# A transformer kernel's first down projection as seven block products, and the split of rounding work between VectorE and GpSimd in both down projections

## What is computed

```python
u = causal_dwconv(hn @ w_up[l], conv_w[l], conv_b[l])       # 1024 x 5632
gate, val = jnp.split(u, 2, axis=-1)
f = (jax.nn.gelu(gate, approximate=True) * val) @ w_down[l] # 1024 x 2816 @ 2816 x 1024
h = h + rms_norm(f, ln_ffn_post[l])
```

## Time and profile before

| | us |
|---|---|
| median of three runs | 2977.24 |
| the profiled execution | 2978.39 |
| its span in the profile | 2976.7 |
| PE busy (matmuls) | 2862.1 |
| DVE busy | 1813.8 |
| ACT busy | 1241.5 |
| POOL busy | 621.2 |

### The profile page before, as it was taken

How to read it: one execution, slowest core, us unless ns; L and a number is a source line. 1 busy time by engine, 2 the same in 40 slices (tenths; PEclk the granted TensorE clock), 3 DMA queues, 4 the chain that set the end, 5 groups by cost and what they waited for, 6 DMA issues and landing times.

```text
span 2976.7 us, 47459 instructions
## 1 busy us (share of the span) xinstructions
PE 2862.1 (96%) x19810; PEld 2299.2 (77%) x19810; DVE 1813.8 (61%) x2296; ACT 1241.5 (42%) x1833; POOL 621.2 (21%) x302
## 2 busy tenths in 40 slices
PE   8999998989899999999899999999899999999999
PEld 6877777777688888888678867766678888888887
DVE  3156768852698889544685545565545766654636
ACT  4145545542545555421453433343433432333334
POOL 4310122221100000344151200000012122244543
PEclk9999999999999999999999999999899999999999
DMA  6433330002422222322345454436543344466664
GB/s 215 153 117 114 121 122 26 27 26 85 142 78 85 85 86 78 121 113 85 115 154 152 152 171 137 125 100 171 193 134 130 120 147 148 156 213 221 224 198 170
DMA packets 283992, 387.84 MB, mean 130 GB/s; under 512 B 12401, under 2 KB 188666, under 8 KB 283778
## 3 DMA queue, kind: packets, MB, share of 16 engines
q1 hardware_dynamic: 268802, 337.60, 35.7%
q10 hardware_dynamic: 14976, 47.19, 4.1%
HBM read 263.34 MB, written 121.41 MB: 129 GB/s over the span
## 4 chain that ended last, share of the span: by engine, by line
PE 85%; DVE 5%; DMA 4%; issue 3%; ACT 2%; SPq 1%; POOL 1%; DVEq 0%; ACTq 0%; POOLq 0%
PE ps L497 25%; PE ps L3284 17%; PE ps L3041 10%; PE ps L2814 9%; PE ps L2110 5%; PE ps L681 4%; PE ps L1530 4%; PE ps L2180 2%; PE ps L2161 2%; PE ps L2138 1%; PE ps L1593 1%; DMA kl<-qk_lo 1%; PE ps L2141 1%; SPq L2471 1%; PE ps L1571 0%
## 5 line engine op out<-in xcount | busy, mean ns | idle before, releaser
L463 POOL TENSOR_TENSOR wl<-wraw,wh 128x1024 fp32r<-128x1024 f32 x62 | 157.4, 2539 | 1119.1 <-ACT wh L458 1109.4
L497 PE MATMUL ps<-xh,wh 128*128 128x512 f32 x752 | 237.8, 398 | 5.2 <-POOL wl L463 2.3
L497 PE MATMUL ps<-xl,wh 128*128 128x512 f32 x752 | 233.7, 392 | 0.0
L497 PE MATMUL ps<-xh,wl 128*128 128x512 f32 x752 | 232.8, 391 | 0.0
L458 ACT ACTIVATE wh<-wraw 128x1024 fp32r<-128x1024 f32 x78 | 82.3, 1056 | 267.7 <-PE ps L497 206.8
L2814 PE MATMUL ps<-gb_hi,ga_hi 128*128 128x512 f32 x448 | 174.9, 390 | 1.6 <-POOL gb_lo L2805 0.8
L497 PEld LDWEIGHTS ps<-xh,wh 128*128 128x128 f32 x752 | 139.6, 189 | 46.7 <-issue 8.6
L2814 PE MATMUL ps<-gb_hi,ga_lo 128*128 128x512 f32 x448 | 174.4, 389 | 0.0
L2814 PE MATMUL ps<-gb_lo,ga_hi 128*128 128x512 f32 x448 | 174.3, 389 | 0.0
L3121 DVE TENSOR_TENSOR y<-ps,y 128x1024 f32<-128x1024 f32 x79 | 96.8, 1225 | 125.6 <-PE ps L497 125.6
L497 PEld LDWEIGHTS ps<-xl,wh 128*128 128x128 f32 x752 | 142.5, 189 | 30.3
(11 more groups left out here) (498 smaller groups left out, 7552.0 us busy)
## 6 DMA issues: line engine op xcount, KB each, us to landing
act_d<-act SPq DMA_DIRECT2D x16, 1792.0 KB, 6.6
ga_raw<-act_d SPq DMA_DIRECT2D x56, 512.0 KB, 4.0
wraw<-in_w_in SPq DMA_DIRECT2D x48, 512.0 KB, 5.0
gb_raw<-in_w_down SPq DMA_DIRECT2D x40, 512.0 KB, 4.9
r_raw<-in_w_up SPq DMA_DIRECT2D x38, 512.0 KB, 3.7
residual<-src ACTq DMA_DIRECT2D x32, 512.0 KB, 5.0
w_raw<-in_w_up SPq DMA_DIRECT2D x32, 512.0 KB, 5.1
proj<-stage SPq DMA_DIRECT2D x30, 512.0 KB, 3.0
```

The costliest lines, as they stand in the source:

```text
L463: nc.gpsimd.tensor_tensor(wl[:, s, :, :], wraw[:, s, :, :], wh[:, s, :, :].bitcast(F32), ALU.subtract).then_inc(w_lo, 1)
L497: mm = nc.tensor.matmul(ps[:, bank + h, :], w, x[:, h * HALF:(h + 1) * HALF], start=start and k == 0, stop=stop and k == 2)
```

## The change

The first down becomes seven block products. The 22 tiles of its inner dimension are 11 pairs (tile k and tile k+11), cut into six chunks of 2, 2, 2, 2, 2 and 1 pairs. That gives 7 x 6 = 42 steps, in which a full step has 24 matmuls and a product's last step 12, together 7 x 11 x 4 x 3 = 924. Steps 0 to 5 are P2, 6 to 11 P1, 12 to 17 P6, 18 to 23 P5, 24 to 29 P7, 30 to 35 P3, 36 to 41 P4. Both downs now use the same functions, and the last two steps are interleaved block by block. Further parts:

- The up's tiles are computed in the order 11, 0, 12, 1, and so on (`F1_TILE`). After each odd one GpSimd makes four 128x512 sums of the two finished tiles (`input_sums1_pool`), and `ff1_gated` waits for earlier ones. SyncE stores three plain blocks and four sums to `act1_d` (7 x 256 KB per pair of tiles, where it was 2 x 512 KB).
- In both downs VectorE makes the low half of the weights and GpSimd that of the inputs; before, it was the other way round in the second down, and GpSimd made both in the first.
- In both downs VectorE makes the weight sums of step i+1 before the low half of step i; before, in the second down, the sums of step i.
- The adding of chunks (`add_one`) falls away: a product's banks are moved out once. The last four squares of the first down are taken by ScalarE from PSUM.
- In the second down the wait for the stored inputs stands once, ahead of step 7's loads, instead of at every P2 step.

```diff
+        def down_load(sp, d, i):
+            name, c = d.steps[i]
+            n, home, loaded = d.kts[c], down_home(d, i), g_loaded[i % 4]
+            if i >= 8 or (i >= 4 and not d.later):
+                sp.wait_ge(down_done, down_done_by(d, i - 4))
...
+        def down_sums_dve(dve, d, i):
+            name, c = d.steps[i]
+            if name not in d.summed:
+                return
...
+            dve.wait_ge(g_loaded[i % 4], down_loaded_by(d, i))
+            if name == "P6":
...
+                    tt(two, raw, two, ALU.add).then_inc(g_sum, 1)
+                    dve.wait_ge(g_sum, at_sums - 1)
+                    tt(one, two, one, ALU.subtract).then_inc(g_sum, 1)
...
+        def down_hi_act(act, d, i):
+            n, home = down_kts(d, i), down_home(d, i)
+            act.wait_ge(g_loaded[i % 4], down_loaded_by(d, i))
+            g_act.done(nc.scalar.activation(home.f_hi[:, 0:n, :], home.f_raw[:, 0:n, :], ACT.Copy), "f")
+            if d.steps[i][0] in d.summed + ("P5",):
+                act.wait_ge(g_sum, down_sums_by(d, i))
+            g_act.done(nc.scalar.activation(home.d_hi[:, 0:n, :], down_weight_source(d, i)[:, 0:n, :], ACT.Copy), "d")
+        def down_lo_dve(dve, d, i):
+            n, home = down_kts(d, i), down_home(d, i)
+            g_act.wait(dve, "d", d.first + i)
+            g_dve.done(nc.vector.tensor_tensor(home.d_lo[:, 0:n, :], down_weight_source(d, i)[:, 0:n, :],
+                                               home.d_hi[:, 0:n, :].bitcast(F32), ALU.subtract), "d")
+        def down_prepare_dve(dve, d, i):
+            if i + 1 < len(d.steps):
+                down_sums_dve(dve, d, i + 1)
+            down_lo_dve(dve, d, i)
+        def down_lo_pool(pool, d, i):
+            n, home = down_kts(d, i), down_home(d, i)
+            g_act.wait(pool, "f", d.first + i)
+            g_pool.done(nc.gpsimd.tensor_tensor(home.f_lo[:, 0:n, :], home.f_raw[:, 0:n, :],
+                                                home.f_hi[:, 0:n, :].bitcast(F32), ALU.subtract), "f")
...
+        def down_products(pe, d, i):
+            name, c = d.steps[i]
+            down_ready_pe(pe, d, i)
             for b in range(4):
+                if c == 0 and name in DOWN_BEFORE:
+                    pe.wait_ge(down_added, down_added_by(d, DOWN_BEFORE[name], b))
+                down_block(d, i, b, c == 0 and name in DOWN_OPENS, c == len(d.kts) - 1).then_inc(down_done, 1)
...
+        def input_sums1_pool(pool, k):
...
+            ff1_dve.wait(pool, "m", 2 * k + 1)
+            if k:
+                pool.wait_ge(act2_stored[1], 32 * k)
...
+            s1_pool.done(tt(t1, b12, b11, ALU.subtract), "T1")
+            s1_pool.done(tt(t3, b22, b12, ALU.subtract), "T3")
+            s1_pool.wait(pool, "T1", k)
+            s1_pool.done(tt(t2, b22, t1, ALU.subtract), "T2")
+            s1_pool.wait(pool, "T2", k)
+            s1_pool.done(tt(t4, b21, t2, ALU.subtract), "T4")
...
@@ the hand-over on ScalarE
-            for m, x in enumerate("gv"):
-                ff1_tap(act, FF_TILES - 1, x)
-                first_copy(act, m)
+            ff1_tap(act, FF_TILES - 1, "g")
+            down_hi_act(act, down1, 1)
+            ff1_tap(act, FF_TILES - 1, "v")
+            down_hi_act(act, down1, 2)
             ff1_gelu(act, FF_TILES - 1)
...
@@ and on VectorE, the last pair and the first down
                 if not more:
+                    down_lo_dve(dve, down1, 0)
                 r7_outputs(dve, ring1, p)
...
+                for k, x in enumerate("gv"):
                     ff1_taps(dve, t, x)
+                    if not more:
+                        down_lo_dve(dve, down1, 1 + k)
                 ff1_gated(dve, t)
...
+            ends = down_ends(down1)
+            for i in range(3, len(down1.steps)):
+                down_prepare_dve(dve, down1, i)
+                if i - 2 in ends:
+                    for b in range(4):
+                        feature_add(dve, down1, ends[i - 2], b)
+            for m in range(4):
+                square_sum_dve(dve, 24 + m)
```

More of the change, by code:

```diff
@@ L78 @@
 U_UP2 = U_OUT2 + KT
-DOWN1 = FF_TILES // 2
-DOWN2_CHUNKS = FF2_TILES // 4
 PAIRS2 = FF2_TILES // 2
@@ new lines, in down_kts, with down_weight_loads, down_loaded_by, down_done_by @@
+        def down_kts(d, i):
+            return d.kts[d.steps[i][1]]
+        def down_weight_loads(d, i):
+            return {"P5": 0, "P6": 2}.get(d.steps[i][0], 1)
+        def down_loaded_by(d, i):
+            s = i % 4
+            whole = sum(16 * (1 + down_weight_loads(e, j)) for e in downs[:downs.index(d)] for j in range(s, len(e.steps), 4))
+            return whole + sum(16 * (1 + down_weight_loads(d, j)) for j in range(s, i + 1, 4))
+        def down_done_by(d, i, b=3):
+            return 4 * (d.first + i) + b + 1
@@ new lines, in down_added_by, with down_sums_by, down_weight @@
+        def down_added_by(d, name, b=3):
+            return 28 * downs.index(d) + 4 * DOWN_PRODUCTS.index(name) + b + 1
+        def down_sums_by(d, i):
+            before = [j for j in range(i + 1) if d.steps[j][0] in d.summed]
+            return d.sums + sum(2 if d.steps[j][0] == "P6" else 1 for j in before)
+        def down_weight(d, k, h, c):
+            r = (k * sum(d.kts) + sum(d.kts[:c])) * P
+            return d.weights[r:r + d.kts[c] * P, h * HALF:(h + 1) * HALF].rearrange("(k p) n -> p k n", p=P)
@@ new lines, in down_block @@
+        def down_block(d, i, b, start, stop):
+            name, home, n = d.steps[i][0], down_home(d, i), down_kts(d, i)
+            t = slice(b * P, (b + 1) * P)
+            f, w = (home.f_hi, home.f_lo), (home.d_hi, home.d_lo)
+            still, moving = (f, w) if d.tokens else (w, f)
+            for kt in range(n):
+                for k, (left, right) in enumerate(((0, 0), (0, 1), (1, 0))):
+                    mm = nc.tensor.matmul(ps[:, DOWN_BANK[name] + b, :], still[left][:, kt, t], moving[right][:, kt, :],
+                                          start=start and kt == 0 and k == 0, stop=stop and kt == n - 1 and k == 2,
@@ new lines, in down_sum_done, with down_ends, feature_add @@
+        def down_sum_done(eng, d, name, b):
+            last = len(d.steps) - 1
+            if name == "P4":
+                eng.wait_ge(down_done, 4 * (d.first + last - 1) + 2 * (b + 1))
+            else:
+                eng.wait_ge(down_done, down_done_by(d, d.steps.index((name, len(d.kts) - 1)), b))
+        def down_ends(d):
+            return {i: name for i, (name, c) in enumerate(d.steps) if c == len(d.kts) - 1 and name != "P4"}
+        def feature_add(dve, d, name, b):
+            row, h = DOWN_TO[name]
+            down_sum_done(dve, d, name, b)
+            part, bank = y[:, 4 * row + b, h * HALF:(h + 1) * HALF], ps[:, DOWN_BANK[name] + b, :]
+            if name in ("P2", "P6", "P5", "P4"):
+                if name == "P4":
+                    dve.wait_ge(x_sq, 24 + 4 + b + 1)
+                ins = nc.vector.tensor_copy(part, bank)
+            else:
+                dve.wait_ge(down_added, down_added_by(d, {"P1": "P2", "P7": "P5", "P3": "P6"}[name], b))
+                ins = nc.vector.tensor_tensor(part, bank, part, ALU.add)
+            ins.then_inc(down_added, 1)
@@ L3701, in _ @@
             for i in range(2):
-                g_lo_pool(pool, i)
+                down_lo_pool(pool, down2, i)
             pair_input_sums(pool, PAIRS2 - 1)
-            for i in range(2, len(DOWN2_STEPS)):
-                g_lo_pool(pool, i)
+            for i in range(2, len(down2.steps)):
+                down_lo_pool(pool, down2, i)
         @block.scalar
@@ L3923, in _ @@
                 else:
-                    g_hi_act(act, 1)
+                    down_hi_act(act, down2, 1)
                 pair_copies(act, p, "c21")
-            for i in range(2, len(DOWN2_STEPS)):
-                g_hi_act(act, i)
+            for i in range(2, len(down2.steps)):
+                down_hi_act(act, down2, i)
             token_roots_act(act)
@@ L3985, in _ @@
             e1_dve.wait(pe, "c12", F1_PAIRS - 2)
-            for c in range(DOWN1):
-                down_products(pe, c, behind=c == DOWN1 - 1)
+            for i in range(len(down1.steps) - 2):
+                if i == len(down1.kts):
+                    e1_act.wait(pe, "c21", F1_PAIRS - 1)
+                    e1_dve.wait(pe, "c12", F1_PAIRS - 1)
+                down_products(pe, down1, i)
+            down_last_products(pe, down1)
             post_sums_pe(pe, 24, KT - 2)
```

513 lines of the change are left out of this document (219 added, 294 removed).

## The result

The changed kernel takes 3005.09 us (median of four runs, 3001.36 to 3007.53), the kernel before 2978.26 beside it: ratio 1.0091, 95% interval 1.0079 to 1.0104. The change makes it slower by 27 us. The profiled execution took 3001.36, its span is 2999.6.

A forecast was written before the change was run, and what follows sets the result against it. It took PE as the bound (busy 96% of the span, 85% of the chain). Terms summed to +15.5 us on 2978.4, giving 2993.9; the median lies 1.15 lower, so forecast 2993 us (chance 0.43), range 2960 to 3010.

The forecast's parts named there:

- Fewer matmuls: First down: 1056 matmuls become 924, 132 fewer at 0.227 us each, -30.0 us.
- Pairs: First up's 19 tile pairs: GpSimd's input sums delay VectorE, so PE loses 1.2 us nine times; +11, ends 0 and 20.
- Steps 1 and 2: First down's start: low halves late by 4.6 and 3.7 us behind VectorE's last-tile work and GpSimd; +8, ends 0 and 9.
- P1 to P6 in the first down: P1's bank copies wait behind step 14's sums and their loads, so PE waits; +12 us, ends 8 and 15.
- Rest of the first down: Low halves of steps 24 and 30 late behind the next step's sums, little elsewhere; +3 us, ends 0 and 5.
- Second down: P1 to P6 +7 us; rest of P6 +2, ends 0 and 4; swap of halves 0, ends -1 and +2.
- End of the first down: VectorE's 0.61 us falls away, but sums and copies stand between last squares: +1, ends -1 and 2; extra traffic 0.
- Clock: Matmuls behind two or three new pauses run at half clock, partly hidden in the pause; +3 us, ends 0 and 6.
- Rival C: Slower still: VectorE becomes the bound of the pairs, busy 364 us; 3002, up to 3010 us; chance 0.16.
- Rival A: Faster: GpSimd's work finds gaps in VectorE's; PE loses nothing if VectorE is under 1.5 us late; 2960 us, chance 0.18.
- Rival B: No change to speak of: the pairs hide GpSimd's work, the downs don't; +4.5, 2982 us, chance 0.18.
- Rival D: The stalls are absent: loads land early enough that neither order nor port matters; -31, 2946 us, chance 0.05.

The follow-up runs named there:

- the kernel with memsets: Changed kernel with GpSimd's four input sums per pair of tiles replaced by memsets of zeros: 2990.1 us, ratio 1.0043 to the kernel before.
- Own sums: Changed kernel, but in both downs VectorE makes step i's weight sums, not step i+1's, before step i's low half: 2987.0 us, ratio 1.0027 to before.
- both back: Own sums, plus VectorE making the inputs' low half and GpSimd the weights' in both downs, on the changed kernel: 2975.9 us, ratio 0.9992 to before.
- held sums: Changed kernel with GpSimd's last two input sums (T2, T4) waiting for VectorE's scaling of the next tile: 3012.0 us, one look.
- P1 copied first: Changed kernel with ScalarE copying P1 out of PSUM ahead of the convolution's tap in every second pair: 2991.8 us, one look.

## Why the prediction was right or wrong

Slower, with 3005 inside the range of 2960 to 3010, was right; the sum of +15.5 was 11 short of +26.7. By its steps:

1. *Fewer matmuls, -30.0*: right. At the 0.2268 us of before (239.5 / 1056) the 924 matmuls are 209.6 us; the other 29.9 of the first down are waits (24.6) and slow clock.
2. *Hand-over, -1.5*: right.
3. *Pairs, +11*: mechanism right in every part (three sums held, 3.1 us together, the tap, the copy of P1, nine times), size short: 1.5 us a time where I had 1.2, 2.0 the first time, and short gaps besides, 15.6. VectorE's scaling starts 3.8 us behind the pair's first matmul, in the kernel with memsets 1.0: it was 2.9 late where I had 2.7, and the slack was 1.4 where I had 1.5.
4. *Steps 1 and 2, +8*: 4.6 and 0.5, against 4.6 and 3.7. VectorE had its low half of step 2 18.9 us after the stage's start, where I had said 19.2. But step 1 itself ran 14 of its 24 matmuls with the clock at 1.2 GHz and took 8.4 us instead of 5.45 (1244.97 to 1253.35), 2.9 more, so that half was ready when it ended. 0.5 and 2.9 are nearly my 3.7. Terms 4 and 9 paid for the same time.
5. *P1 to P6 in the first down, +12*: 14.2, in the range, by a chain other than mine. I let the sums of step 14 wait for their load; in fact VectorE was behind already, with the second sum of step 13 (3.27) and the low half of step 12 (3.38), and four turns of some 2.1 us each were lost, not three.
6. *Rest of the first down, +3*: 5.3 (1.6 at step 11, 1.5 at step 15 in P6, 1.2 at step 26 in P7, 0.9 at step 32 in P3; not at steps 24 and 30, where I had put it). That a look-ahead also catches the last step of P1 wasn't in my sum.
7. *Second down, +7, +2 and 0*: 12.6 with the clock; waits alone 5.4 more ahead of P6 and 1.7, 1.8 and 1.3 elsewhere, less the 0.5 that one step waited before, 9.7. The step that failed is "the swap of halves itself: 0". I weighed durations (1.2 behind 2.4 for 2.4 behind 1.2), not when each half can start. Own sums show the swap at +8.3 us over before when alone. The sum came near only because the two costs overlap.
8. *End of the first down, +1*: from the start of its last matmul to that of the second block's first product it is 11.2 us against 12.0, -0.8, near the low end. (This lies outside the stages and is not in the sum below.) Traffic at 0: right, as both back and the memset in the pairs show.
9. *Clock, +3*: what is left of the stages behind the waits is 5.3 us in the first down (29.9 less 24.6) and 2.9 in the second (12.6 less 9.7), 8.2; 28 matmuls that start 0.43 us apart are 5.6 of it. Mis-sized, beyond the 6 that I gave as its end; I had discounted the slow time for being hidden, which only that of term 4 was.

Together: -31.5 + 15.6 + 5.1 + 14.2 + 5.3 + 9.7 + 8.2 = 26.6. So the forecast of a loss stands by its mechanism, but its size rests in part on luck: term 7 had the swap at nothing, and the clock cost almost three times what I gave it. Rival C named the time but only part of the cause: VectorE was busy for 337 of 357 us, and of the 15.6 us that the pairs lost, moving the copy of P1 gave back 7.3; the rest came out as gaps at P1 and P7. Rival A's point of decision (VectorE under 1.5 us late) was the right place to look: it was 2.9 late there. Rival B fell with the 15.6 us of the pairs. Rival D's -31 would need a first down of 210 us; the best here is 222.5.

## What to carry to other kernels

In these traces work handed to an idle GpSimd cost VectorE up to the length of GpSimd's instruction (2.1 of 2.4 us) wherever VectorE's instruction had two inputs in SBUF and GpSimd's read SBUF. So a plan for it must say beside what it falls: a PSUM read or an idle stretch is free, a sum on the critical list is not. When two engines share out halves, compare when each half's input is ready, not what it lasts. And each wait added to one engine's list must be followed into every queue that consumes it, SyncE's included: two held sums made the pairs 11 us longer through a store that stood ahead of a load.

## What was unexpected on the hardware

- With work queued on both, VectorE and GpSimd go strictly in turns: 3.3 us for each VectorE instruction of 1.2 (1.28 for a tap), four in a row ahead of P6, and neither gets two turns running. Whether the taps take part, had left open; they do (6.72 us for two). By the Trainium skill (SBUF — State Buffer, "Who interferes with whom") they have to, having two inputs in SBUF, and the trace agrees.
- Short waits were enough for the clock. In the kernel with P1 copied first, a wait of 2.0 us at 1328 in P6 was followed by seven matmuls 0.43 us apart. The wait of 2.6 us at step 1 was followed by seven or eight such in four kernels and by none in two. In the pairs of the kernel with the held sums a wait of 3.0 us was followed by seven, and seven waits of 2.3 to 2.8 us by none. Behind waits of 1.9 us or less there were none, and behind those of 4.2 us and more there were five to thirteen. So between these a wait's length alone did not settle it.
- The stretch between the downs, 5756 matmuls with the same code in all fourteen kernels, took 1188.8 to 1196.2 us in their profiles, 1196.1 in that of before and 1191.3 in that of after. A single profile's span can't settle a few microseconds. The first down, with the same code in five of them, still moved from 239.5 to 243.3. What stays open is why.
